# A routing table built by accumulating indirect DMAs instead of one-hot matmuls, in a fused two-block transformer kernel

## The chip, the cores and the metric

The kernel runs on one core of a Trainium2 chip. The metric is the device time of one launch in microseconds (us). The kernel before takes 1685.63 us, the median of three runs (1685.04 to 1687.07).

## The reference, cut to what matters

The program computes one block with a recurrent mixer and an expert layer (PEER), followed by two blocks with attention and a feed-forward layer, for 256 tokens of width 1024, in f32. The change lies in the expert layer. For each token and each of 8 heads, two lists of 128 key scores are cut to their top 16, the 256 sums of pairs are cut to the top 16 again, and a softmax over these gives 16 weights with 16 expert numbers out of 128 * 128.

```
q = (t @ w_q).reshape(n_tok, 8, 2, 128)
sc = einsum("thpk,hpnk->thpn", q, sub_keys)
s_top, i_top = top_k(sc, 16)
cand = s_top[:, :, 0, :, None] + s_top[:, :, 1, None, :]
cand_idx = i_top[:, :, 0, :, None] * 128 + i_top[:, :, 1, None, :]
best, pos = top_k(cand.reshape(n_tok, 8, 256), 16)
idx = take_along_axis(cand_idx.reshape(n_tok, 8, 256), pos)
g = softmax(best)
act = gelu(einsum("phkd,pd->phk", u_tab[idx], t))
out = einsum("phk,phkd->pd", g * act, v_tab[idx])
```

A token uses at most 128 of 16384 experts. The kernel computes all of them densely: with a table W of weights, 128 x 128 x 256 (second index j, first index i, token), mostly zero, the layer is the sum over j of V_j times (W_j * gelu(U_j x)). A block j holds 128 experts; U_j and V_j are 128 x 1024 each.

## The kernel before, in words

**Products.** A matmul operand is split into a rounded part (`high`, made by ScalarE in `take_high`, L823) and the rest (`low`, made by VectorE in `take_low`, L1748), and a product is three matmuls. A piece of weights is 128 x 1024 (512 KB). Pieces go through a ring of four slots (`raw`, `high`, `low`): SyncE's `load` (L612) waits for the `low` of the piece four before, `ahead(p)` on ScalarE and VectorE makes the parts of the piece four after p, and TensorE signals `slot_done`. The order of all pieces is `STREAM`. Each engine executes its instructions, and each queue its issues, in the order written, so a wait holds up all behind it.

**Up to the scores.** The mixer runs in 8 rounds over 8 pieces each. VectorE's `finish` (L1887 to L1890) ends a round (`merged_ready`). Then 8 pieces of `mix_out`, a norm (add L1990, squares L804, transposes L1245), and 16 pieces of `query` in four rounds `it`, of two heads each. In a round the four query projections are followed by 8 score matmuls (L1386), and VectorE does the top-k work of the round (L2030 to L2096) after the lows of the four pieces ahead.

**U blocks before the table.** 24 `NATIVE` blocks run as plain f32 matmuls (L1398) between the rounds, from buffers of their own. 36 `STAGED` blocks run through the ring (`project_in`, L1255 to L1257), 4 before and 32 during the making of the table. Their activations gelu(U_j x) wait in the arena.

**The table.** W is made for 4 tokens at a time in 64 groups: VectorE (L2116, L2121), ScalarE (L976, L982) and GpSimd (L770) build one-hot matrices, and TensorE multiplies them (L1423), 4 matmuls of 128 x 128 a group. ScalarE copies the result to the arena (L998), or VectorE multiplies it into stored activations.

**Experts.** In `expert_step` the other 68 (`LATE`) blocks do V_j (`project_out`, L1305 to L1309) and U_(j+3) (`project_in_halves`, L1275 and L1277) in turn, with a sum (L2163), a gelu (L1017), a multiplication by the table (L2167) and the split of the product (L1025, L1758) for each; 60 more steps do V alone. After the last V comes a norm and the rest of the network.

Of the kernel before, what the change touches and what calls it, by code (L numbers as in the profile page):

```python
# [67 lines left out]
EARLY_OF_ROUND = (4, 4, 4, 12)  # L68
NATIVE = sum(EARLY_OF_ROUND)
LEAD, STAGED = 4, 36  # L70
FIRST_NATIVE = NKEYS - NATIVE
EARLY = NATIVE + STAGED
LATE = NKEYS - EARLY
GROUPS = SEQ // 4
# [6 lines left out]
class Chain:  # L81
# [28 lines left out]
    def link(self, ins):  # L110
# [4 lines left out]

STREAM = [("mix", 8 * KC), ("mix_out", KC), ("query", 16), ("staged", STAGED), ("expert", NKEYS + LATE),
          ("diff_v", KC), ("diff_qk", 16), ("diff_out", KC), ("ffn0", 3 * FF_CHUNKS),
# [70 lines left out]
def piece_staged(k):  # L188

    return Piece("staged", k)  # L190


def staged_block(k):

    return FIRST_NATIVE - 1 - k


def first_staged(n):

    return FIRST_NATIVE - LEAD - n // 2  # L200


def piece_u(j, it=0):

    return Piece("expert", j if j < 3 else 2 * j - 2, it, 8)


def piece_v(j, it=0):

    return Piece("expert", 2 * j + 3, it, 8) if j < LATE - 3 else Piece("expert", j + LATE, it, 4)  # L210
# [28 lines left out]
def build(nc, x, w_mix, w_gate, w_out, w_query, keys, u_tab, v_tab, diff_qk, diff_v, diff_out,  # L239
# [3 lines left out]
    with ctx:  # L243
# [5 lines left out]


# [100 lines left out]
        def weights_of(n, j, j_end):  # L351

            return arena[:, :].rearrange("p (j t) -> p j t", t=SEQ)[:, j:j_end, 4 * n:4 * n + 4].rearrange("p j t -> p t j")

        def coefficients(j, it):

            return coef[j % 2] if j < LATE else at(arena, it * (4 * SEQ) + j * SEQ, SEQ)

        def staged_part(k, lo, hi):

            return part(staged_block(k) * SEQ + lo, hi - lo)

        def staged_bank(k, lo, hi):

            return bank(4 + k % 4, lo, hi - lo)

        def scattered(n):

            return bank(n % 4).rearrange("p (t j) -> p t j", t=4)
# [13 lines left out]
        one_hot = [h_tok[:, 512 * n:512 * n + 512] for n in range(2)]  # L383
        one_hot_w = [h_tok[:, 1024 + 512 * n:1536 + 512 * n] for n in range(2)]
        coef = [h_tok[:, SEQ * n:SEQ * n + SEQ] for n in range(2)]
        u_sum = [h_tok[:, 512 + SEQ * n:512 + SEQ * n + SEQ] for n in range(2)]
        weight = spare[:, :]
        minus_weight = params[:, 0:GROUPS]
        sel_i, sel_j = (yh[:, SEQ * n:SEQ * n + SEQ].bitcast(F32) for n in range(2))

        filler = part(8192, HALF)
# [2182 lines left out]
```

## Time and profile before

| what | us or share |
|---|---|
| median of three runs | 1685.63 |
| time of the profiled execution's span | 1683.6 |
| difference (outside the span, and between executions) | 2.0 |
| TensorE busy | 99% |
| VectorE busy | 77% |
| ScalarE busy | 55% |
| GpSimd busy | 7% |
| granted TensorE clock, mean | 0.999 of 2.4 GHz |

The profiled execution has no other time of its own than its span. PE is TensorE, DVE is VectorE, ACT is ScalarE, POOL is GpSimd, SP is SyncE. The end of a matmul is modelled, and consecutive matmuls overlap, so the pace of TensorE is read from starts and not from durations.

### The profile page before, as it was taken

The page shows a single profiled execution, that of the slowest core. Times are in us where ns is not written, and L with a number is a line of the kernel's source. Part 1 is how long each engine was busy: PE and PEld are TensorE (multiplying, and loading weights), DVE is VectorE, ACT ScalarE, POOL GpSimd, SP SyncE. Part 2 cuts the span into 40 slices and gives each one's busy share as a digit, 9 for nine tenths or more (in the row PEclk, how much of TensorE's full clock was granted, in tenths as well). Part 3 has the DMA queues.
Part 4 walks back from the last instruction along what each step waited for, and adds up shares of the span by engine and source line. Part 5 has one row for each costly group of instructions (what it writes and reads, how often), then busy time and mean ns, then how long its engine had stood idle before and what let it go on. Part 6 is the DMA issues. An engine that isn't in the chain of part 4 may idle for free.

```text
span 1683.6 us, 28949 instructions
## 1 busy us (share of the span) xinstructions
PE 1665.7 (99%) x10094; PEld 1470.5 (87%) x10094; DVE 1302.4 (77%) x2459; ACT 931.8 (55%) x1625; POOL 109.8 (7%) x94
## 2 busy tenths in 40 slices
PE   9999999999999999999999999999999999999998
PEld 8999899999998888888888888898888878888886
DVE  7888789989997666666666666687877877687777
ACT  5666632268875444444444545565655545655554
POOL 1000000035550000000000000010000000000000
PEclk9999999999999999999999999999999999999999
DMA  6556733523336555555556567544665645266663
GB/s 218 181 181 202 251 128 133 197 75 114 113 111 212 187 187 188 188 186 187 188 187 191 193 195 254 166 134 152 201 187 187 200 160 164 89 200 188 187 187 112
DMA packets 84601, 292.96 MB, mean 174 GB/s; under 512 B 11696, under 2 KB 13488, under 8 KB 84144
## 3 DMA queue, kind: packets, MB, share of 16 engines
q1 hardware_dynamic: 82800, 286.54, 52.3%
q10 hardware_dynamic: 1728, 5.45, 0.9%
q8 instruction: 45, 0.74, 0.2%
q14 instruction: 28, 0.23, 0.1%
HBM read 289.33 MB, written 2.10 MB: 173 GB/s over the span
## 4 chain that ended last, share of the span: by engine, by line
PE 87%; issue 7%; DVE 4%; ACT 1%; POOL 0%; DMA 0%; POOLq 0%; DVEq 0%; ACTq 0%
PE ps L1275 16%; PE ps L1305 10%; PE ps L1307 10%; PE ps L1309 10%; PE ps L1277 8%; PE ps L1255 7%; PE ps L1256 7%; PE ps L1257 7%; PE ps L1398 5%; PE ps L1423 3%; PE ps L1288 1%; DVE low L1748 1%; DVE held_low L1748 0%; DVE arena L1817 0%; PE ps L1386 0%
## 5 line engine op out<-in xcount | busy, mean ns | idle before, releaser
L1748 DVE TENSOR_TENSOR low<-raw,high 128x1024 fp32r<-128x1024 f32 x492 | 591.3, 1209 | 184.5 <-ACT high L823 177.6
L823 ACT ACTIVATE high<-raw 128x1024 fp32r<-128x1024 f32 x493 | 513.8, 1046 | 304.4 <-PE ps L1309 132.0
L1275 PE MATMUL ps<-x_parts,high 128*128 128x512 f32 x1216 | 432.9, 398 | 0.0
L1277 PE MATMUL ps<-x_parts,low 128*128 128x256 f32 x1216 | 341.2, 281 | 0.0
L1255 PE MATMUL ps<-x_parts,low 128*128 128x256 f32 x1104 | 317.4, 288 | 1.4 <-DVE x_parts L1864 0.9
L1257 PE MATMUL ps<-x_parts,high 128*128 128x256 f32 x1104 | 312.2, 283 | 0.0
L1256 PE MATMUL ps<-x_parts,high 128*128 128x256 f32 x1104 | 312.2, 283 | 0.0
L1275 PEld LDWEIGHTS ps<-x_parts,high 128*128 128x128 f32 x1216 | 228.4, 188 | 55.1
L1277 PEld LDWEIGHTS ps<-x_parts,low 128*128 128x128 f32 x1216 | 229.5, 189 | 4.0
L1255 PEld LDWEIGHTS ps<-x_parts,low 128*128 128x128 f32 x1104 | 211.5, 192 | 4.1 <-issue 1.4
L1256 PEld LDWEIGHTS ps<-x_parts,high 128*128 128x128 f32 x1104 | 211.6, 192 | 0.1
L1257 PEld LDWEIGHTS ps<-x_parts,high 128*128 128x128 f32 x1104 | 211.5, 192 | 0.0
L1305 PE MATMUL ps<-high,yl 128*128 128x512 f32 x640 | 199.8, 393 | 0.1
L1307 PE MATMUL ps<-low,yh 128*128 128x512 f32 x640 | 198.9, 392 | 0.0
L1309 PE MATMUL ps<-high,yh 128*128 128x512 f32 x640 | 197.3, 389 | 0.0
L1307 PEld LDWEIGHTS ps<-low,yh 128*128 128x128 f32 x640 | 120.1, 188 | 27.6
L1309 PEld LDWEIGHTS ps<-high,yh 128*128 128x128 f32 x640 | 120.1, 188 | 27.0
L1305 PEld LDWEIGHTS ps<-high,yl 128*128 128x128 f32 x640 | 112.9, 188 | 22.3 <-DVE yl L1758 0.5
L770 POOL TENSOR_SCALAR h_tok<-consts,yh,spare 128x128 f32<-128x128 f32 x64 | 87.4, 1372 | 209.0 <-ACT yh L969 149.8
L754 POOL TENSOR_TENSOR stats<-stats 128x1 f32<-128x1 f32 x14 | 7.9, 565 | 1268.0 <-DVE stats L1789 1268.0
L1398 PE MATMUL ps<-arena 128*128 128x256 f32 x384 | 83.5, 379 | 0.0
L1398 PEld LDWEIGHTS ps<-arena 128*128 128x128 f32 x384 | 72.7, 190 | 9.7
(352 smaller groups left out, 2022.3 us busy)
## 6 DMA issues: line engine op xcount, KB each, us to landing
raw<-in_v_tab SPq DMA_DIRECT2D x128, 512.0 KB, 3.4
raw<-in_u_tab SPq DMA_DIRECT2D x104, 512.0 KB, 3.5
raw<-in_ffn_in SPq DMA_DIRECT2D x88, 512.0 KB, 4.1
raw<-in_w_mix SPq DMA_DIRECT2D x56, 512.0 KB, 4.5
raw<-in_ffn_out SPq DMA_DIRECT2D x44, 512.0 KB, 3.5
arena<-in_u_tab SPq DMA_DIRECT2D x24, 512.0 KB, 3.6
raw<-in_w_query SPq DMA_DIRECT2D x16, 512.0 KB, 5.3
raw<-in_diff_qk SPq DMA_DIRECT2D x16, 512.0 KB, 4.3
```

The costliest lines, as they stand in the source:

```text
L770: pool.tensor_scalar(one_hot_w[n % 2][:, 3 * PARTS:4 * PARTS], iota, sel_j[:, t:t + 1], weight[:, t:t + 1], ALU.is_equal, ALU.mult).then_i ...
L823: a.activation(w_high(p, 0, n), cols(raw, p, 0, n), ACT.Copy).then_inc(slot_high[p.slot], 1)
L1255: pe.matmul(dst, left[1], right[0], start=start, stop=False)
L1256: pe.matmul(dst, left[0], right[1], start=False, stop=False)
L1257: return pe.matmul(dst, left[0], right[0], start=False, stop=stop)
L1275: pe.matmul(bank(b).rearrange("p (h t) -> p h t", h=2), cols(high, p, k * PARTS, PARTS), both[:, :, k, :], start=(k == 0), stop=False)
L1277: ins = pe.matmul(bank(b, 0, SEQ), cols(low, p, k * PARTS, PARTS), chunk_of(xh, k), start=False, stop=(k == KC - 1))
L1305: pe.matmul(bank(2 * t + half), src_low[:, xs], w_high(p, half * HALF, HALF), start=first, stop=False)
L1307: pe.matmul(bank(2 * t + half), src_high[:, xs], w_low(p, half * HALF, HALF), start=False, stop=False)
L1309: ins = pe.matmul(bank(2 * t + half), src_high[:, xs], w_high(p, half * HALF, HALF), start=False, stop=stop)
L1398: ins = pe.matmul(bank(4 + early % 4, 0, SEQ), early_u[early % 4][:, k * PARTS:(k + 1) * PARTS], chunk_of(xf, k), start=(k == 0), stop=(k ...
L1748: v.tensor_tensor(w_low(p, 0, n), cols(raw, p, 0, n), w_high(p, 0, n).bitcast(F32), ALU.subtract).then_inc(slot_low[p.slot], 1)
```

## The change

The one-hot matrices, their matmuls, the native blocks and the staged blocks go. A DRAM tensor `routed` (128 x 128 x 256 f32, 16.8 MB) takes the table. GpSimd clears it during the mixer with 32 DMAs of 512 KB, four after each `merged_ready`. VectorE makes in each top-k round the flat index and the weight of each chosen expert (32 per token and round). GpSimd adds them with one indirect DMA for each head, token tile and rank: 256 DMAs, each of 128 single f32 elements, one per partition. Before a head of one token tile, it waits until all DMAs of that tile's earlier heads have landed (two heads may choose the same expert). 64 U blocks run through the ring with `project_in`, 16 behind the four queries of each round, and VectorE's `ahead` calls are written between the steps of the top-k. 64 more U blocks follow with `project_in_halves` (`inner_step`). All 128 V blocks follow all U blocks (`outer_step`), and SyncE loads a 128 KB part of the table for each, after it has waited for all 256 indirect DMAs. The load of the keys (1 MB) moves on SyncE's queue from before `mix_out` to behind it, after a wait for the last `merged_ready`, and so ahead of the query pieces; the store of `h` moves ahead of the U pieces. The softmax is done in each round and not once. The buffer `xf` and its addition (L2011) go.

```
-EARLY_OF_ROUND = (4, 4, 4, 12)
-LEAD, STAGED = 4, 36
+ROUNDS, OF_ROUND = 4, 16
+EARLY = ROUNDS * OF_ROUND
+SCRATCH = 44
+SLOTS = HEADS * 16
+ZERO_PARTS = 32
...
+def block_of(k):
+    return k + SCRATCH if k < NKEYS - SCRATCH else k - (NKEYS - SCRATCH)
```

On SyncE:

```
-            sp.dma_start(keysT, keys).then_inc(keys_loaded, 16)
             for k in range(KC):
                 load(Piece("mix_out", k), w_out[k])
+            sp.wait_ge(merged_ready, KC)
+            sp.dma_start(keysT, keys).then_inc(keys_loaded, 16)
+            for it in range(ROUNDS):
                 for q in range(4 * it, 4 * it + 4):
+                    load(piece_query(q), w_query[q])
                 if it == 0:
                     sp.wait_ge(h_ready, TB)
                     sp.dma_start(h_saved, h_tok[:, :]).then_inc(h_kept, 16)
+                for k in range(it * OF_ROUND, (it + 1) * OF_ROUND):
+                    load(piece_u(k), u_tab[block_of(k)])
...
+            def outer_step(j, it):
                 load(piece_v(j, it), pick(v_tab, it * 4 + j))
+                if j == 0:
+                    for b in range(TB):
+                        sp.wait_ge(scattered[b], 16 * SLOTS)
+                if j >= 4:
+                    sp.wait_ge(coef_ready, it * 4 + (j - 3))
+                sp.dma_start(routed_part[j % 4], pick(routed, it * 4 + j)).then_inc(routed_loaded[j % 4], 16)
```

On GpSimd:

```
+            for c in range(KC):
+                pool.wait_ge(merged_ready, c + 1)
+                for n in range(c * ZERO_PARTS // KC, (c + 1) * ZERO_PARTS // KC):
+                    pool.dma_start(cleared[n], zeros).then_inc(zeroed, 16)
             inverse_roots(1, 2)
+            pool.wait_ge(zeroed, 16 * ZERO_PARTS)
+            for h in range(HEADS):
+                if h % 2 == 0:
+                    pool.wait_ge(chosen_ready, h // 2 + 1)
+                for b in range(TB):
+                    if h >= 1:
+                        pool.wait_ge(scattered[b], 16 * 16 * h)
+                    for n in range(b * SLOTS + 16 * h, b * SLOTS + 16 * h + 16):
+                        pool.indirect_dma_start(entries, bass.IndirectOffsetOnAxis(ap=slot_index[:, n:n + 1], axis=0),
+                                                slot_weight[:, n:n + 1], None, compute_op=ALU.add).then_inc(scattered[b], 16)
```

On TensorE:

```
+            for it in range(ROUNDS):
                 for q in range(0 if it else 2, 4):
+                    project_in(piece_query(4 * it + q), bank(4 + q, 0, SEQ))
+                for k in range(it * OF_ROUND, (it + 1) * OF_ROUND):
+                    project_in(piece_u(k), bank(4 + k % 4, 0, SEQ))
+                    if k % OF_ROUND == 0:
...
+            def inner_step(k, it):
+                project_in_halves(piece_u(k, it), 4 + k % 4)
+            def outer_step(j, it):
                 pe.wait_ge(coef_low, it * 4 + (j + 1))
                 if j < NKEYS - HOLD:
+                    project_out(piece_v(j, it), *y_parts(j, NKEYS), 0, first=(j == 0))
```

On ScalarE, in each round:

```
+                for k in range(it * OF_ROUND, (it + 1) * OF_ROUND):
+                    ahead(piece_u(k))
+                    gelu_early(k)
+                    if k % OF_ROUND == OF_ROUND - 2:
+                        a.wait_ge(shifted_ready, it + 1)
+                        w = slot_weight3[:, :, 32 * it:32 * it + 32]
+                        a.activation(w, w, ACT.Exp).then_inc(exp_ready, 1)
```

On VectorE in each round, behind the top-k steps with `ahead(u[0])` to `ahead(u[14])` between them, and then the new steps behind all rounds:

```
+                    ins = v.tensor_scalar(first, first, 2.0 * PARTS, token[:, b:b + 1], ALU.mult, ALU.add)
+                v.wait_ge(exp_ready, it + 1)
+                link(v.tensor_reduce(sums.rearrange("p (b h) -> p b h", b=TB), weights4, AX.X, ALU.add))
+                link(v.reciprocal(sums, sums))
+                    v.scalar_tensor_tensor(out=index3[:, b, heads], in0=second, scalar=2.0 * PARTS * PARTS, in1=first, op0=ALU.mult, op1=ALU.add)
+                    ins = v.tensor_tensor(weights4[:, b], weights4[:, b], sums[:, 2 * b:2 * b + 2].unsqueeze(2).to_broadcast([PARTS, 2, 16]), ALU.mult)
+                ins.then_inc(chosen_ready, 1)
...
+            def inner_step(k, it):
+                v.tensor_reduce(u_sum[k % 2], halves(4 + k % 4), AX.X, ALU.add).then_inc(u_summed, 1)
+                if k in (NKEYS - 2, NKEYS - 1):
+                    coef_low_part(k - (NKEYS - 2))
+                ahead(p)
+                if k in (NKEYS - 4, NKEYS - 3, NKEYS - 2):
+                    weigh(k - (NKEYS - 4))
+            def outer_step(j, it):
                 if j + 2 < NKEYS:
                     coef_low_part(j + 2, it)
+                if j < NKEYS - 2:
                     ahead(piece_v(j, it))
+                if j + 3 < NKEYS:
+                    weigh(j + 3, it)
```

## Rows read from the trace of the kernel before

**Rows 1.** The page: busy time by engine, then the granted clock in 40 slices.

```profile
PE 1665.7 (99%) x10094; PEld 1470.5 (87%) x10094; DVE 1302.4 (77%) x2459; ACT 931.8 (55%) x1625; POOL 109.8 (7%) x94
...
PEclk9999999999999999999999999999999999999999
```

**Rows 2.** Windows: stretch, its length, busy PE, PEld, DVE, ACT, POOL, clock, DMA share, GB/s.

```profile
25.00:180.00 155.00, 155.00 (x1293) 154.87 (x1291) 136.19 (x244) 104.39 (x154) 0.00 (x0) 1.00 0.58 192
180.00:220.00 40.00, 39.23 (x238) 34.65 (x239) 28.60 (x50) 23.78 (x43) 1.10 (x2) 1.00 0.66 231
220.00:357.00 137.00, 136.53 (x836) 126.26 (x835) 129.73 (x472) 40.82 (x75) 1.26 (x1) 1.00 0.41 143
357.00:507.00 150.00, 149.94 (x1283) 149.51 (x1282) 144.12 (x317) 125.00 (x285) 86.12 (x64) 1.00 0.34 109
507.00:860.00 353.00, 353.00 (x1774) 296.88 (x1773) 243.48 (x321) 172.94 (x254) 0.00 (x0) 1.00 0.59 190
```

**Rows 3.** TensorE's timeline: start, us, line, tile, count; boundaries of blocks.

```profile
220.01 1.95 PE L1386 MATMUL ps<-arena 128*128 128x128 f32 x16
221.80 1.03 PE L1398 MATMUL ps<-arena 128*128 128x256 f32 x4
...
345.22 0.39 PE L1255 MATMUL ps<-x_parts,low 128*128 128x256 f32 x1 [0.47 <-ACT arena L946]
...
353.95 0.82 PE L1410 MATMUL ps<-consts,arena 128*128 128x128 f32 x6
...
507.39 0.40 PE L1275 MATMUL ps<-x_parts,high 128*128 128x512 f32 x1
...
515.87 0.63 PE L1305 MATMUL ps<-high,yl 128*128 128x512 f32 x2
...
655.66 0.64 PE L1305 MATMUL ps<-high,yl 128*128 128x512 f32 x2
...
658.45 0.39 PE L1275 MATMUL ps<-x_parts,high 128*128 128x512 f32 x1
...
1034.88 0.62 PE L1305 MATMUL ps<-high,yl 128*128 128x512 f32 x2
...
1037.60 0.62 PE L1305 MATMUL ps<-high,yl 128*128 128x512 f32 x2
...
1052.16 0.63 PE L1305 MATMUL ps<-high,x_parts 128*128 128x512 f32 x2
```

**Rows 4.** Groups of the page: busy us, mean ns of one.

```profile
L1748 DVE TENSOR_TENSOR low<-raw,high 128x1024 fp32r<-128x1024 f32 x492 | 591.3, 1209 | 184.5 <-ACT high L823 177.6
...
L770 POOL TENSOR_SCALAR h_tok<-consts,yh,spare 128x128 f32<-128x128 f32 x64 | 87.4, 1372 | 209.0 <-ACT yh L969 149.8
L754 POOL TENSOR_TENSOR stats<-stats 128x1 f32<-128x1 f32 x14 | 7.9, 565 | 1268.0 <-DVE stats L1789 1268.0
...
L1398 PE MATMUL ps<-arena 128*128 128x256 f32 x384 | 83.5, 379 | 0.0
```

**Rows 5.** Groups of the window 355 to 506 us.

```profile
L1423 PE MATMUL ps<-h_tok 128*128 128x128 f32 x512 | 62.5, 275 | 0.0
...
L1748 DVE TENSOR_TENSOR low<-raw,high 128x1024 fp32r<-128x1024 f32 x32 | 38.8, 1213 | 0.0
```

**Rows 6.** VectorE's timeline, second top-k round and lows of the next.

```profile
259.76 1.64 DVE L2030 MAX8 arena<-arena 128x8 f32<-128x128 f32 x8
...
287.32 4.62 DVE L1748 TENSOR_TENSOR low<-raw,high 128x1024 fp32r<-128x1024 f32 x4
```

**Rows 7.** GpSimd's one-hot line: duration in ns, min, median and max.

```profile
L770 POOL TENSOR_SCALAR h_tok<-consts,yh,spare x64: 787/1382/2293, 355.7 to 500.8; 128x128 f32<-128x128 f32 x64
```

**Rows 8.** DMA issues: count, KB each, median us from issue to landing.

```profile
raw<-in_w_query SPq DMA_DIRECT2D x16, 512.0 KB, 5.3
...
raw<-in_w_gate SPq DMA_DIRECT2D x8, 128.0 KB, 2.8
arena<-in_keys SPq DMA_DIRECT2D x1, 1024.0 KB, 7.4
...
spare<-in_forget_bias SPq DMA_DIRECT2D x2, 8.0 KB, 3.6
```

**Rows 9.** Timeline before the norm: SyncE's issues, VectorE, ScalarE.

```profile
186.24 7.65 SPq L612 DMA_DIRECT2D raw<-in_w_query  x4
...
189.31 0.43 DVE L1890 SCALAR_TENSOR_TENSOR arena<-arena 128x256 f32<-128x256 f32 x1
...
191.99 1.99 ACT L823 ACTIVATE high<-raw 128x1024 fp32r<-128x1024 f32 x2
...
193.44 2.35 DVE L1748 TENSOR_TENSOR low<-raw,high 128x1024 fp32r<-128x1024 f32 x2
...
196.20 1.37 DVE L1990 SCALAR_TENSOR_TENSOR h_tok<-ps,h_tok 128x512 f32<-128x512 f32 x2 [0.41 <-PE ps L1302]
```

More of the change, by code:

```diff
@@ L184, in later, with piece_query, piece_u @@
         return p
[L188 to L205, printed above, removed]
+def piece_query(q):
+    return Piece(f"query{q // 4}", q % 4)
+def piece_u(k, it=0):
+    return Piece(f"early{k // OF_ROUND}", k % OF_ROUND) if k < EARLY else Piece("inner", k - EARLY, it, 4)
+def block_of(k):
+    return k + SCRATCH if k < NKEYS - SCRATCH else k - (NKEYS - SCRATCH)
 def piece_v(j, it=0):
-    return Piece("expert", 2 * j + 3, it, 8) if j < LATE - 3 else Piece("expert", j + LATE, it, 4)
+    return Piece("outer", j, it, 4)
 def piece_gate(l, n, it=0):
@@ L425, in build @@
         best = part(7744, 64)
-        sel = part(7808, 3 * SEQ)
+        chosen = part(7808, 2 * 64)
         expsum = part(8576, 32)
-        early_u = [part(9216 + D * n, D) for n in range(4)]
-        xf = part(13312, KC * SEQ)
         v_tok = part(0, TB * D)
@@ L1011, in _ @@
[L1011 to L1022 removed]
+                if it == 1:
+                    a.wait_ge(zeroed, 16 * ZERO_PARTS)
@@ new lines, in _ @@
+                    ahead(u[12 + 2 * n])
+                    chain.wait()
+                    chain.step(v.tensor_tensor(eqs4, eqs4, idx4[:, :, n, :].unsqueeze(2).to_broadcast([PARTS, 4, 16, 16]), ALU.mult))
+                    if n == 0:
+                        ahead(u[13])
+                    chain.wait()
+                    chain.step(v.tensor_reduce(places4[:, n], eqs4, AX.X, ALU.add))
+                chain.wait()
+                for b in range(TB):
+                    first, second = (chosen[:, 64 * n + 32 * b:64 * n + 32 * b + 32] for n in range(2))
+                    ins = v.tensor_scalar(first, first, 2.0 * PARTS, token[:, b:b + 1], ALU.mult, ALU.add)
@@ new lines, in _ @@
+                chain.step(ins)
+                v.wait_ge(exp_ready, it + 1)
+                sums = expsum[:, 0:4]
+                link(v.tensor_reduce(sums.rearrange("p (b h) -> p b h", b=TB), weights4, AX.X, ALU.add))
+                link(v.reciprocal(sums, sums))
+                for b in range(TB):
+                    first, second = (chosen[:, 64 * n + 32 * b:64 * n + 32 * b + 32] for n in range(2))
+                    v.scalar_tensor_tensor(out=index3[:, b, heads], in0=second, scalar=2.0 * PARTS * PARTS, in1=first, op0=ALU.mult, op1=ALU.add)
+                    ins = v.tensor_tensor(weights4[:, b], weights4[:, b], sums[:, 2 * b:2 * b + 2].unsqueeze(2).to_broadcast([PARTS, 2, 16]), ALU.mult)
```

573 lines of the change are left out of this document (195 added, 378 removed).

## The prediction

> **What bounds the kernel now.** I read the page first: TensorE is busy 99% of the span, at full clock in every slice [rows 1]. A busy TensorE need not be a TensorE at its pace, so I then read windows by stage: its share is full from 25 us to 860 us, VectorE's reaches 144 of 150 us while the table is made, and the 16 DMA engines are busy 34% to 66% [rows 2]. Last I read the pace from starts [rows 3]. The reader is to see that blocks follow each other without gaps, so that the time of the expert layer is the sum of TensorE's blocks, from the first score matmul at 220.01 to the first matmul of the next stage at 1052.16: 832.2 us.
>
> **What TensorE does in the 832.2 us.** From [rows 3]: three `project_in` blocks take 353.95 - 345.22 = 8.73, so 2.91 each; three `project_in_halves` blocks 515.87 - 507.39 = 8.48, so 2.83; a V block among U blocks 658.45 - 655.66 = 2.79, and among V blocks 1037.60 - 1034.88 = 2.72. A round's scores take 221.80 - 220.01 = 1.79. The native blocks take 83.5 [rows 4], 3.48 each. The one-hot matmuls take 62.5 by the group's busy time [rows 5]; with their overlaps out, the table stage of 150 us [rows 2] less its 32 staged blocks (93) leaves 57.
>
> **The change on TensorE.** The new order holds 4 * 1.79 = 7.2 of scores, 12 queries and 64 early U blocks at 2.91 (221.2; the first round's four queries lie before 220.01), 64 U blocks at 2.83 (181.1) and 128 V blocks. Among V blocks alone 2.72 applies: 348.2. VectorE has 0.42 more to do there for each V (the multiplication by the table), some 2.1 us of 2.72, and ScalarE 1.5, so they hide. The sum is 757.7, and the saving 832.2 - 757.7 = 74.5. It consists of 57 for the one-hots, 24 * (3.48 - 2.91) = 14 for the native blocks, and small terms. With V at 2.79 it is 65.
>
> **VectorE in a round.** A round on TensorE is 20 * 2.91 + 1.79 = 60.0. VectorE's top-k work is 287.32 - 259.76 = 27.6 [rows 6]. The new index and softmax steps, some ten short ones, I estimate at 2 from that stretch. 20 lows at 1.21 [rows 4] are 24.2. The sum, 53.8, fits into 60.0. Following the order step by step, with scores ready 6 us after the fourth query (one U block, the scores, ScalarE's copies), each low comes 2 us or more before TensorE needs it, the tightest being those for the next round's queries. So the round costs no stall, and its chosen slots are ready about 53 us after the fourth query. If that cover goes, each us too much costs 4 us in four rounds.
>
> **The moved key load, a cost.** The keys now wait on SyncE for the last `merged_ready`, and the four query loads stand behind them. The last `finish` ends at 189.7, where SyncE issued the first query at 186.24 [rows 9]. ScalarE and VectorE split queries 0 and 1 (191.99 and 193.44) in their order before the norm's first add at 196.20, so a late query holds up the norm, on which TensorE waits. Queued now at 189.7 are 1 MB of keys, 1 MB of two queries, and beside them the last 2 MB of clearing. Below: query 1 lands 5.3 after its issue at 190.5 [rows 8], its split takes 2.3, and VectorE is free at 198.1, 2 late. Above: 4 MB at the rate that 231 GB/s in a 0.66 share makes for full engines, 350 [rows 2], takes 12, and with a latency of 2 and the split VectorE is free at 206, 10 late. I take 6.
>
> **Clearing.** 32 * 0.52 = 16.8 MB in the mixer add about 95 GB/s to 192 in a share of 0.58 [rows 2], so 0.87. Loads have several us of lead there. I take 1, with 0 and 10 as ends. GpSimd has nothing else to do then but two small steps of the norm, and the first of these comes behind the add at 196.20, over 6 us after the last clears can start.
>
> **The scatter, the unknown.** The trace before has no DMA from GpSimd. Work that must be done: 256 DMAs. The first 64 can begin at 53 us after the fourth query. TensorE ends all U blocks 7.2 + 221.2 + 181.1 = 409 after it. From the last landing to the first V there are the table's load (2.8, as the 128 KB gate load, [rows 8]) and what VectorE and ScalarE have queued around `weigh(0)`, about 5 (two sums, two lows, the splits). The last DMA itself lands in about 2.8. So there are 409 - 53 - 5 - 2.8 - 2.8 = 345 us for 256, or 1.35 each, and everything above goes one to one into the end. Later rounds leave more: 64 DMAs in the last 185 us. The waits for earlier heads hide, as 16 DMAs of the other tile lie between.
>
> What is one DMA's price c on GpSimd? Below: a GpSimd instruction on one column took 0.565 [rows 4]. Above: one at a time from issue to landing, 2.8 [rows 8]; then 256 take 717, and V starts 372 late. Between them lies the 128-column one-hot, 1.37 beside a VectorE that is hardly ever idle [rows 7]. A column of 128 entries is nearer to the small instruction in data, but 128 descriptors are more work than one pass; I take 1.2, so 307 us and no stall. On the DMA engines 128 packets of a few bytes are little: the 8 KB broadcast landed in 3.6, against 2.8 for 128 KB [rows 8].
>
> **A rule that speaks against it.** The one-hot on GpSimd took between 0.79 and 2.29 for the same work [rows 7], so something held it up for over a us at times. The Trainium skill (SBUF — State Buffer, section "SBUF: two separate sides") states that GpSimd and VectorE share a port pair as an exclusive lock, and that descriptors of a DMA from GpSimd can't be written while VectorE holds it in a 2-port mode; a VectorE op with two SBUF inputs blocks only GpSimd ops that read SBUF. By that the spread agrees, and whether an indirect DMA counts as reading is open. The Trainium skill (DMA: Bandwidth & Descriptors, section "Anatomy of one DMA — SWDGE (gpsimd) path") fits 2.0 us for one small DMA, mostly receipt; were that paid in series, V would start 167 us late and the time be 1785.
>
> **The sum.** -74.5 + 6 + 1 = -67.5. The span before is 1683.6, so 1616.1; the median stands 2.0 above that span, so 1618. 0.2% is 3.4 us, about what a measurement of this kernel can tell from no change.
>
> **The rivals.**
> - A partly late scatter: c between 1.35 and 1.61. The stall is 256c - 345, and the gain is used up at (345 + 67.5) / 256 = 1.61. For it: the one-hot's 1.37 [rows 7] gives a stall of 6 and 1624; c = 1.5 gives 39 and 1657.
> - A scatter that sets the time: c above 1.61, the case on the other side. The mechanism is one DMA's descriptor work on GpSimd, held up by VectorE. In the inner stage VectorE runs one two-operand low of 1.21 in each block of 2.83; if GpSimd gets only the remaining 1.62, my 1.2 becomes 2.1, 538 us in all, a stall of 193 and 1811. At c = 2.0 it is 167 and 1785. For it: the spread of [rows 7]. Against: an indirect DMA reads a single column, and VectorE was busy 144 of 150 us there [rows 2], while in the inner stage a sum and a low make about 1.9 of 2.83.
> - VectorE as the bound in the rounds: with 0.5 us more for each of its 25 large ops in a round (20 lows, 5 of the top-k) the 53.8 become 66, 6 over the 60.0, or 24 in four rounds, and 1642. Against: the low was no longer beside GpSimd's work (1.21 in the table stage [rows 5] and 1.21 over all [rows 4]).
> - That the change does not remove the work cannot be: the one-hots and natives are gone from the program, and TensorE has nothing hidden to put in their place.
>
> **How the numbers follow.** Forecast (c up to 1.35): 0.50, with a range of its own from 1606 to 1628. Partly late: 0.12, of which 0.09 is faster and 0.03 within 0.2%. VectorE bound: 0.05, faster. Scatter bound: 0.33, slower. So faster 0.64, same 0.03, slower 0.33. The range begins at 1606 (no cost of the key load and of clearing, 1611, and a shade for faster V blocks), and ends at 1760, which is c = 1.9; above lie 0.17 and below 0.03.
>
> **What would show it.** Right: V starts at about 636 us in the new trace (220 + 409 + 7), with no gap of TensorE before it; rounds 60 us apart; the last indirect DMA lands before 628; the gap before the norm's transposes grows by 6; V blocks 2.72 apart. Wrong: SyncE waits for GpSimd at `outer_step(0)`, TensorE idle between the last U and the first V, and GpSimd's DMAs back to back all the way from the first round. Then the price c has failed, not the sum of the blocks. If TensorE waits for lows in the rounds, the VectorE sum has failed.

## The result and the profile after

The changed kernel takes 1918.99 us (1917.12 to 1919.34, 4 runs) beside 1685.97 (4 runs) of the kernel before. The ratio is 1.138, 95% interval [1.136, 1.139]: slower. The forecast was 1618, with a range up to 1760, so the forecast and its range both missed. Below, a time without a range is that of one run; runs of one kernel lie 2 to 4 us apart here. The profiled execution has a span of 1915.3 us, 231.7 more than before.

The page of the changed kernel: busy time of engines, then tenths by slice, what it gives of the chain, and the group of the indirect DMAs. It answers to [rows 1].

```profile
PE 1633.3 (85%) x9800; PEld 1405.8 (73%) x9800; DVE 1244.2 (65%) x2274; ACT 878.6 (46%) x1431; POOL 537.7 (28%) x319
PE   9999799999999500006999999999999999999998
POOL 1100007888888888881000000000100000000000
PEclk9999999999999855557999999999999999999999
PE 28%; POOL 26%; issue 19%; DVE 12%; ACT 9%; DMA 4%; ACTq 1%; DVEq 1%; SPq 0%; POOLq 0%
L752 POOL DMA_INDIRECT routed<-h_tok x256 | 497.1, 1942 | 145.0 <-issue 77.8
```

TensorE has a hole of four slices and its clock falls in them to 0.5, the lower of its two levels; GpSimd, which had next to nothing to do, is on the chain of waits with 26% of the span. Its 256 indirect DMAs take 1.94 us each, and 77.8 us more go by between them ("issue", 0.30 each). Where the hole lies, TensorE's timeline shows, with the boundaries of its stages (it answers to [rows 3]):

```profile
243.79 1.95 PE L1313 MATMUL ps<-arena 128*128 128x128 f32 x16
...
879.24 1.22 PE L1222 MATMUL ps<-high,yl 128*128 128x512 f32 x2 [231.26 <-DVE yl L1640]
...
886.25 0.61 PE L1222 MATMUL ps<-high,yl 128*128 128x512 f32 x2
887.61 0.61 PE L1222 MATMUL ps<-high,yl 128*128 128x512 f32 x2
...
1283.05 0.63 PE L1222 MATMUL ps<-high,x_parts 128*128 128x512 f32 x2
```

The first scores start at 243.79; one U block of 2.91 lies ahead of them, so the fourth query ends at 240.9. The U blocks end at 879.24 - 231.26 = 647.98, the V stage lasts from 879.24 to 1283.05. The releaser named is VectorE's `yl`, but VectorE stood idle too; who waited for what is in SyncE's list of waits:

```profile
SPq L647 <- DMA routed<-h_tok: 239.4, 1, 239.4
```

SyncE waits at `outer_step(0)` for the last indirect DMA before it loads the first block of the table. The windows (PE, weight loads, VectorE, ScalarE, GpSimd, then clock, DMA share, GB/s; they answer to [rows 2]) are those of the mixer, the rounds, the U blocks after the rounds, the hole, and the V blocks:

```profile
25.00:210.00 185.00, 177.23 (x1376) 172.16 (x1375) 148.16 (x264) 113.58 (x168) 17.25 (x32) 0.99 0.72 257
240.00:480.00 240.00, 240.00 (x1972) 238.26 (x1972) 205.95 (x558) 125.36 (x183) 162.83 (x77) 1.00 0.67 178
480.00:640.00 160.00, 160.00 (x908) 138.68 (x907) 108.68 (x114) 76.87 (x113) 142.94 (x57) 1.00 0.66 180
700.00:869.00 169.00, 0.00 (x0) 0.00 (x0) 0.00 (x0) 0.00 (x0) 141.08 (x92) 0.50 0.24 0
900.00:1200.00 300.00, 290.31 (x1157) 209.23 (x1156) 190.78 (x288) 131.15 (x192) 0.00 (x0) 1.00 0.68 210
```

In the U stage TensorE is as full as foretold; in the hole nothing runs but GpSimd; and in the V blocks TensorE's share is under the whole, which is a second loss. GpSimd's counts say how fast the scatter goes: 57 DMAs in 160 us, 92 in 169 us. The ranges of their durations (ns: min, median, max) by stretch:

```profile
L752 POOL DMA_INDIRECT routed<-h_tok x77: 1536/2320/3150, 294.0 to 479.7; - x77
L752 POOL DMA_INDIRECT routed<-h_tok x60: 1543/2522/2592, 479.7 to 645.5; - x60
L752 POOL DMA_INDIRECT routed<-h_tok x108: 1543/1543/1562, 669.5 to 867.3; - x108
```

With all other engines idle one takes 1.54, beside the U blocks after the rounds 2.52, and in the rounds anything from 1.54 to 3.15. With the gaps of 0.30 that is one per 1.85 us alone, (479.7 - 294.0) / 77 = 2.41 in the rounds, and (647.98 - 479.7) / 60 = 2.80 after them, which is very nearly one per U block.

**Where the 231.7 us come from.** The span was to be 1616.1 and is 1915.3, 299.2 more. The terms, each measured less foretold:

| | foretold | measured | off by |
|---|---|---|---|
| fourth query ends later than before by | 7 | 240.9 - 220.0 = 20.9 | +13.9 |
| U stage | 409 | 407.1 | -1.9 |
| TensorE idle ahead of the first V | 0 | 231.3 | +231.3 |
| V stage | 348.2 | 403.8 | +55.6 |
| the rest, to the end | 631.4 | 632.3 | +0.9 |

They add up to 299.8. Against before, the same terms are 20.9 + (407.1 + 231.3 + 403.8 - 832.2) + 0.9 = 231.8.

**The V stage.** ScalarE and VectorE, timelines of one block of the changed kernel:

```profile
1003.12 0.42 ACT L948 ACTIVATE yh<-arena 128x256 fp32r x1 [1.72 <-DVE arena L2024]
1003.45 1.04 ACT L805 ACTIVATE high<-raw 128x1024 fp32r<-128x1024 f32 x1
1006.21 0.42 ACT L948 ACTIVATE yh<-arena 128x256 fp32r x1 [1.72 <-DVE arena L2024]
...
1003.58 0.42 DVE L1640 TENSOR_TENSOR yl<-arena,yh 128x256 fp32r<-128x256 f32 x1 [0.57 <-ACT yh L948]
1004.52 1.23 DVE L1630 TENSOR_TENSOR low<-raw,high 128x1024 fp32r<-128x1024 f32 x1 [0.52 <-ACT high L805]
1005.67 0.42 DVE L2024 TENSOR_TENSOR arena<-arena,h_tok 128x256 f32 x1
```

Both engines are idle for part of each block, and still they set the pace: ScalarE's `yh` waits for the multiply by the table (L2024), the weight's high part follows it on ScalarE, the low (L1630) waits for that, and the multiply stands behind the low in VectorE's order. One turn of this loop is 1006.21 - 1003.12 = 3.09 here, and a V block takes 3.13 on average, where TensorE needs 2.72.

**The start.** The norm's first add and the split ahead of it, and the group of weight splits on ScalarE between 25 and 215 us with what it waited for; it answers to [rows 9]:

```profile
214.17 1.06 ACT L805 ACTIVATE high<-raw 128x1024 fp32r<-128x1024 f32 x1 [2.77 <-DMA raw<-in_w_query]
...
216.40 1.28 DVE L1875 SCALAR_TENSOR_TENSOR h_tok<-ps,h_tok 128x512 f32<-128x512 f32 x2
...
L805 ACT ACTIVATE high<-raw 128x1024 fp32r<-128x1024 f32 x55 | 56.8, 1054 | 67.5 <-DMA raw<-in_w_mix 33.0 <-PE ps L1174 23.2 <-DMA raw<-in_w_query 8.8
```

The add comes at 216.40, 20.2 after its place in [rows 9]. ScalarE waits 8.8 us for the queries (the price foretold for the key load was 6, between 2 and 10), but also 33.0 us for the mixer's own weights, whose loads run beside the clearing; some 12 of these reach the end, as the mixer's last `finish` ends at 201.9 and not at 189.7.

### The profile page after: what moved, and what is told of

Same layout as the page of the kernel before. It is cut to its first block, busy times and chain, and to the rows that moved or that the text cites. A ratio compares the mean times of both kernels' runs of the same rounds, so it can differ in the third digit from the quotient of the medians.

```text
span 1915.3 us, 28883 instructions
## 1 busy us (share of the span) xinstructions
PE 1633.3 (85%) x9800; PEld 1405.8 (73%) x9800; DVE 1244.2 (65%) x2274; ACT 878.6 (46%) x1431; POOL 537.7 (28%) x319
## 4 chain that ended last, share of the span: by engine, by line
PE 28%; POOL 26%; issue 19%; DVE 12%; ACT 9%; DMA 4%; ACTq 1%; DVEq 1%; SPq 0%; POOLq 0%
POOL routed L752 26%; PE ps L1192 8%; ACT high L805 7%; PE ps L1194 4%; DVE arena L2024 3%; DVE low L1630 3%; PE ps L1222 2%; PE ps L1224 2%; PE ps L1226 2%; DMA raw<-in_w_mix 2%; PE ps L1172 2%; PE ps L1174 2%; PE ps L1173 2%; PE ps L1205 1%; DMA raw<-in_w_query 1%
## 5 line engine op out<-in xcount | busy, mean ns | idle before, releaser
L805 ACT ACTIVATE high<-raw 128x1024 fp32r<-128x1024 f32 (+1 forms) x517 | 536.8, 1044 | 543.5 <-DMA raw<-in_v_tab 234.3
L1630 DVE TENSOR_TENSOR low<-raw,high 128x1024 fp32r<-128x1024 f32 (+1 forms) x516 | 621.7, 1210 | 175.7 <-ACT high L805 171.5
L752 POOL DMA_INDIRECT routed<-h_tok x256 | 497.1, 1942 | 145.0 <-issue 77.8
L1192 PE MATMUL ps<-x_parts,high 128*128 128x512 f32 x1184 | 419.6, 398 | 0.0
L1172 PE MATMUL ps<-x_parts,low 128*128 128x256 f32 x1328 | 379.1, 285 | 8.0 <-DVE low L1630 7.1
L1173 PE MATMUL ps<-x_parts,high 128*128 128x256 f32 x1328 | 376.4, 283 | 0.0
L1174 PE MATMUL ps<-x_parts,high 128*128 128x256 f32 x1328 | 376.3, 283 | 0.0
L1194 PE MATMUL ps<-x_parts,low 128*128 128x256 f32 x1184 | 332.3, 281 | 0.0
L1172 PEld LDWEIGHTS ps<-x_parts,low 128*128 128x128 f32 x1328 | 255.4, 192 | 10.8 <-DVE low L1630 8.1
L1192 PEld LDWEIGHTS ps<-x_parts,high 128*128 128x128 f32 x1184 | 222.4, 188 | 54.7
L1173 PEld LDWEIGHTS ps<-x_parts,high 128*128 128x128 f32 x1328 | 255.5, 192 | 0.0
L1174 PEld LDWEIGHTS ps<-x_parts,high 128*128 128x128 f32 x1328 | 255.4, 192 | 0.0
L1194 PEld LDWEIGHTS ps<-x_parts,low 128*128 128x128 f32 x1184 | 223.6, 189 | 1.5
L2024 DVE TENSOR_TENSOR arena<-arena,h_tok 128x256 f32 (+1 forms) x128 | 53.7, 419 | 230.4 <-DMA h_tok<-routed 230.4
L948 ACT ACTIVATE yh<-arena 128x256 fp32r (+1 forms) x124 | 51.9, 418 | 214.5 <-DVE arena L2024 211.7
```

The lines of the kernel that those rows point to most:

```text
L752: pool.indirect_dma_start(entries, bass.IndirectOffsetOnAxis(ap=slot_index[:, n:n + 1], axis=0), slot_weight[:, n:n + 1], None, compute_op ...
L805: a.activation(w_high(p, 0, n), cols(raw, p, 0, n), ACT.Copy).then_inc(slot_high[p.slot], 1)
L1172: pe.matmul(dst, left[1], right[0], start=start, stop=False)
L1173: pe.matmul(dst, left[0], right[1], start=False, stop=False)
L1174: return pe.matmul(dst, left[0], right[0], start=False, stop=stop)
L1192: pe.matmul(bank(b).rearrange("p (h t) -> p h t", h=2), cols(high, p, k * PARTS, PARTS), both[:, :, k, :], start=(k == 0), stop=False)
```

## Experiments

Three losses had to be told apart: the scatter, the order in the V stage, and the start.

**The order of the V stage.** `v_order` swaps two steps of VectorE:

```diff
             def outer_step(j, it):
                 if j + 2 < NKEYS:
                     coef_low_part(j + 2, it)
-                if j < NKEYS - 2:
-                    ahead(piece_v(j, it))
                 if j + 3 < NKEYS:
                     weigh(j + 3, it)
+                if j < NKEYS - 2:
+                    ahead(piece_v(j, it))
```

> Only VectorE's order in the V steps is changed: the multiplication by the table stands before the low of the piece ahead. In the changed kernel a V block takes 3.08 us. Theory A: this is a loop of ScalarE and VectorE (split of the product, rounded part of the piece, its low, the multiplication, and back to the split: 0.42 + 1.04 + 1.23 + 0.42 us), and the order breaks it: V blocks 2.72 apart, 128 * 0.36 = 46 less, about 1873. Rival B: the table's loads or memory make TensorE slower; then V stays at 3.08 and the time at 1919.

Measured: 1870.26 us (1868.79 to 1871.91), ratio 1.110 [1.108, 1.111]. TensorE's timeline and window in the V stage of `v_order`:

```profile
882.40 1.22 PE L1222 MATMUL ps<-high,yl 128*128 128x512 f32 x2 [231.13 <-DVE yl L1640]
...
1234.71 0.63 PE L1222 MATMUL ps<-high,x_parts 128*128 128x512 f32 x2
...
900.00:1200.00 300.00, 300.00 (x1325) 248.43 (x1324) 219.09 (x331) 150.61 (x221) 0.00 (x0) 1.00 0.76 243
```

The stage takes 352.3 us instead of 403.8, TensorE is full in it, and VectorE's busy time has gone up with the pace: it was never short of time. Only the order of two steps differs, so the loop was the cause. The price of 2.72 per V holds in this order (348.2 foretold; about 2.9 of the other 4.1 are the slow first matmuls below).

**The scatter left out.** `few_adds` issues 16 of the 256 indirect DMAs, the first one of each head and tile:

```diff
                     if h >= 1:
-                        pool.wait_ge(scattered[b], 16 * 16 * h)
-                    for n in range(b * SLOTS + 16 * h, b * SLOTS + 16 * h + 16):
+                        pool.wait_ge(scattered[b], 16 * h)
+                    for n in range(b * SLOTS + 16 * h, b * SLOTS + 16 * h + 1):
```

> Leaves out 240 of the 256 indirect DMAs (the table misses 15 of 16 entries). Theory A: the wait for them is all that they cost, so the 231 us of TensorE's wait go and the first V comes within 1 us of the last U; V blocks stay at 3.08; time 1919 - 231 = 1687. Rival B: the adds also slow the U blocks or the loads; then the U stage of 407 us gets shorter too, and the time falls below 1680.

Measured: 1684.53 us. TensorE's first V matmul in `few_adds`:

```profile
647.68 0.62 PE L1222 MATMUL ps<-high,yl 128*128 128x512 f32 x2
```

V follows U without a gap, the U stage is as long as with 256 DMAs, and a V block still takes 3.13 us on average. So the scatter costs TensorE nothing but the hole: 1919 - 1684.5 = 234.5 us for 231.3 us of it and the clock behind it.

**What one indirect DMA costs: its entries.** `half_rows` gives each DMA 64 entries instead of 128, at the same count:

```diff
-bass.IndirectOffsetOnAxis(ap=slot_index[:, n:n + 1], axis=0), slot_weight[:, n:n + 1]
+bass.IndirectOffsetOnAxis(ap=slot_index[0:64, n:n + 1], axis=0), slot_weight[0:64, n:n + 1]
```

> Each indirect DMA takes the first 64 partitions only (half of the table's entries are left out). An indirect DMA takes 1.54 us on GpSimd while VectorE is idle, plus 0.30 to the next. Theory A: the time is descriptors, one per entry, so it falls to 0.8 to 1.0, and beside VectorE's work to 1.7 or less; the wait for the adds falls from 231 to below 60. Rival B: a fixed cost of the instruction, then it stays above 1.4 and the time is 1900 or more.

Measured: 1838.46 us. Durations in `half_rows` in the hole, and in the U blocks after the rounds:

```profile
L752 POOL DMA_INDIRECT routed<-h_tok x72: 1407/1411/1426, 665.1 to 786.8; - x72
L752 POOL DMA_INDIRECT routed<-h_tok x85: 1407/1411/1990, 478.6 to 638.8; - x85
```

Half the entries save 0.13 of 1.54 us. A line through these two points, an estimate, gives 2 ns for each entry and some 1.3 us that no entry changes. By the duration theory A has fallen. Yet the time fell by 80 us, where rival B had 19 at most and 256 * 0.13 is 34: after the rounds the median went from 2.52 to 1.41, as if alone. So it was not the amount of work beside them that had made them 2.52 long; something there hung on a period. That became the question. Whether fewer DMAs with more entries each would be cheaper is not shown: a kernel with 16 of them, of 16 columns each, gave no time.

**What holds a DMA up: operations of VectorE.** `vector_in_wait` puts three kinds of operations of VectorE into the hole, each linked to the one before:

```diff
                 ahead(p)
+                if k == NKEYS - 4:
+                    for _ in range(60):
+                        link(v.tensor_tensor(yl[:, :], xh[:, 0:HALF].bitcast(F32), xl[:, 0:HALF].bitcast(F32), ALU.add))
+                    for _ in range(130):
+                        link(v.tensor_copy(spare[:, :], xh[:, 0:SEQ].bitcast(F32)))
+                    for _ in range(60):
+                        link(v.tensor_tensor(yl[:, :], bank(0), xl[:, 0:HALF].bitcast(F32), ALU.add))
```

> Adds work to VectorE in the stretch in which it waits for the table and nothing is loaded: 60 additions of two SBUF operands (128 x 512, 0.69 us each), then 130 copies SBUF to SBUF (128 x 256), then 60 additions of a PSUM and an SBUF operand (128 x 512). The results are not used. In the changed kernel an indirect DMA takes 1.54 us there, against 2.5 beside VectorE's lows. Theory A: a port that GpSimd shares with VectorE is held, so the DMA gets longer beside at least one of the three kinds, to 2 us or more, first of all beside two SBUF operands as in the lows. Rival B: it was the loads of weights on the same DMA engines; then it stays at 1.54 beside all three.

Measured: 1925.37 us. The durations in `vector_in_wait` beside the sums of two SBUF operands, beside the copies, and beside the sums with one operand in PSUM; then the copies' own durations:

```profile
L752 POOL DMA_INDIRECT routed<-h_tok x17: 1874/1875/1877, 649.5 to 684.4; - x17
L752 POOL DMA_INDIRECT routed<-h_tok x26: 1550/1550/1882, 686.6 to 733.3; - x26
L752 POOL DMA_INDIRECT routed<-h_tok x22: 1542/1542/1543, 735.1 to 773.9; - x22
...
L2043 DVE COPY spare<-x_parts x130: 293/295/465, 687.0 to 734.8; 128x256 f32<-128x256 f32 x130
```

Of the three kinds only the sums of two SBUF operands hold an indirect DMA up, and all DMAs beside them are of one length, 1.87 (theory A had said 2 or more). Each ends 1.42 after the end of the sum in which it began. The sums that read PSUM hold up nothing: 1.54, at whatever point of a sum a DMA begins. By this, where the rule of the Trainium skill (SBUF — State Buffer, section "SBUF: two separate sides") left open whether an indirect DMA counts as a GpSimd operation that reads SBUF, it behaves as one that does.

The copies show less than that. Beside them a DMA takes 1.55, but the two run in step: a DMA starts every 1.86 us, in which just five copies pass, and always 0.02 after the start of a copy. So only this one meeting was tried, and in it the copies are the ones that get longer: 25 of the 130 take 0.45 or more where most take 0.29, about one for each DMA. The warning of the same section of the Trainium skill that copies of fp32 within SBUF keep GpSimd from writing descriptors is thus neither shown nor refuted; the copies here are short, and longer ones were not run.

**What holds a DMA up: traffic.** `loads_in_wait` has SyncE copy 60 blocks of `u_tab` within DRAM during the hole, two at a time.

```diff
                 if j == 0:
+                    for n in range(60):
+                        if n >= 2:
+                            sp.wait_ge(copied[n % 2], 16 * (n // 2))
+                        sp.dma_start(junk[n], u_tab[n]).then_inc(copied[n % 2], 16)
                     for b in range(TB):
                         sp.wait_ge(scattered[b], 16 * SLOTS)
```

> Adds 60 DMAs of 512 KB from the U table to an unused DRAM tensor on SyncE's queue, two at a time, in the stretch in which VectorE and all loads are idle. Theory A (VectorE's port): an indirect DMA stays at 1.54 us beside them. Rival B (DMA engines or memory): it rises to 2.3 us or more.

Measured: 1919.94 us. Window and durations in `loads_in_wait`:

```profile
660.00:860.00 200.00, 0.00 (x0) 0.00 (x0) 0.00 (x0) 0.00 (x0) 167.01 (x109) 0.50 0.63 131
...
L758 POOL DMA_INDIRECT routed<-h_tok x109: 1542/1542/1561, 660.0 to 859.6; - x109
```

With the DMA engines at a share of 0.63, about that of the U stage (0.66), the indirect DMAs take 1.54 as before. Traffic is not it, as far as copies within DRAM can stand for loads into SBUF; `split_lows` below has these loads beside DMAs of 1.54.

**Is it a phase lock?** The timelines of GpSimd and VectorE in the changed kernel, after the rounds:

```profile
561.67 2.46 POOL L752 DMA_INDIRECT routed<-h_tok  x1 [0.30 <-issue]
564.43 2.58 POOL L752 DMA_INDIRECT routed<-h_tok  x1 [0.30 <-issue]
...
561.48 1.23 DVE L1630 TENSOR_TENSOR low<-raw,high 128x1024 fp32r<-128x1024 f32 x1 [0.31 <-ACT high L805]
...
564.37 1.23 DVE L1630 TENSOR_TENSOR low<-raw,high 128x1024 fp32r<-128x1024 f32 x1 [0.37 <-ACT high L805]
```

A DMA starts 0.19 after a low has begun and ends 1.42 after that low's end (564.13 against 562.71); the next starts 0.30 later, at 564.43, just after the next low has begun at 564.37, and is held up again. A DMA alone needs 1.54 + 0.30 = 1.84 of the 2.83 of a block, but the low delays each one by just so much that the next meets the next low. The rule holds beyond this pair: after 480 us 57 DMAs are held up, and all 57 end 1.41 to 1.44 after the low that was running when they began. The DMA of 64 entries, 0.13 shorter, slips out: it starts before the next low, and a low that begins behind it does not hold it up.

The same trace tells about the rounds, where VectorE has the top-k steps too. Of the 77 DMAs there 21 take 1.54, and 49 end 1.41 to 1.44 after the end of an operation with two SBUF operands: 43 after a low, 6 after a step of the top-k (L1997, L2000). The three of 3.15 all begin in the top-k's sum L1958 and outlast also the low behind it:

```profile
323.65 3.15 POOL L752 DMA_INDIRECT routed<-h_tok  x1 [0.30 <-issue]
...
322.90 1.21 DVE L1958 TENSOR_TENSOR arena<-arena 128x1024 f32<-128x1024 f32 x1
324.02 1.22 DVE L1630 TENSOR_TENSOR low<-raw,high 128x1024 fp32r<-128x1024 f32 x1
```

If a DMA after the rounds is held up because it meets the low of each block, a shorter low should free the whole one too. `query_first` is the base for this; it also takes back part of the start:

```diff
+            for q in range(2):
+                load(piece_query(q), w_query[q])
             sp.wait_ge(merged_ready, KC)
             sp.dma_start(keysT, keys).then_inc(keys_loaded, 16)
             for it in range(ROUNDS):
-                for q in range(4 * it, 4 * it + 4):
+                for q in range(4 * it if it else 2, 4 * it + 4):
```

> The V order of before, and the loads of queries 0 and 1 ahead of the wait and the keys on SyncE's queue. Theory A: the norm's first add no longer waits for query 1 (its load landed 14 us late), 8 us less than with the V order alone, the rest of the later start being the clearing: 1865. Rival B: the last clears alone hold the queries up, then it is within 3 us of the V order alone.

Measured: 1863.45 us, 6.8 less than `v_order`, near theory A's 8: first scores at 241.05, and ScalarE's waits for queries down to 4.7. `split_lows` takes that kernel and makes two lows of each in the U stage; `parted_lows` does so after the rounds only, with the block's sum from PSUM between the halves. The edit of `split_lows`:

```diff
                 v.wait_ge(slot_high[p.slot], p.count)
-                v.tensor_tensor(w_low(p, 0, n), cols(raw, p, 0, n), w_high(p, 0, n).bitcast(F32), ALU.subtract
-                                ).then_inc(slot_low[p.slot], 1)
+                first = 0
+                if start_of("query0") <= p.n < start_of("outer"):
+                    first = HALF
+                    v.tensor_tensor(w_low(p, 0, first), cols(raw, p, 0, first), w_high(p, 0, first).bitcast(F32), ALU.subtract)
+                v.tensor_tensor(w_low(p, first, n - first), cols(raw, p, first, n - first), w_high(p, first, n - first).bitcast(F32), ALU.subtract
+                                ).then_inc(slot_low[p.slot], 1)
```

> In the U stage every low of 1,024 columns on VectorE becomes two of 512, back to back; otherwise query_first (1863.5 us). Theory A: an indirect DMA reads its index only when VectorE is not in an operation on two SBUF operands, and with one low per block it falls into step with the lows, one DMA per block of 2.82 us. If the short pause between two operations back to back is enough, a DMA is held up for at most 0.65 us, ends before the next low and gets out of step: period about 2.1 us in the stretch after the rounds, some 75 DMAs where there were 57, and about 1830 us. If the pause is not enough, nothing changes (2.52 us each, 1863). Rival B: the longer DMAs of that stretch come from the stage's traffic, and the lows only mark its beat: no change either, here and in parted_lows.

> In the blocks after the rounds the low is two of 512 columns with the sum of 512 columns from PSUM (0.69 us) between them; otherwise query_first (1863.5 us). Theory A: each half holds a DMA up for at most 0.65 us and the sum from PSUM for nothing, so that it gets out of step with the blocks: mean period 2.1 to 2.3 us in that stretch, 70 to 78 DMAs for 57, and 1825 to 1840 us. Rival B (the traffic of the stage makes them 2.5 us long): still 57 DMAs and 1863 us.

Measured: `split_lows` 1799.44 us, `parted_lows` 1815.11. Durations from 480 to 640 us in `query_first`, `split_lows` and `parted_lows`, in this order:

```profile
L754 POOL DMA_INDIRECT routed<-h_tok x57: 2451/2524/2592, 479.8 to 638.1; - x57
```

```profile
L754 POOL DMA_INDIRECT routed<-h_tok x85: 1542/1543/2184, 479.8 to 639.6; - x85
```

```profile
L754 POOL DMA_INDIRECT routed<-h_tok x84: 1542/1542/1907, 479.3 to 639.6; - x84
```

Timelines of GpSimd and VectorE in `split_lows`, in a round and after the rounds:

```profile
309.59 2.46 POOL L754 DMA_INDIRECT routed<-h_tok  x1 [0.30 <-issue]
...
563.59 1.71 POOL L754 DMA_INDIRECT routed<-h_tok  x1 [0.30 <-issue]
...
309.37 0.67 DVE L1635 TENSOR_TENSOR low<-raw,high 128x512 fp32r<-128x512 f32 x1
309.96 0.68 DVE L1636 TENSOR_TENSOR low<-raw,high 128x512 fp32r<-128x512 f32 x1
...
563.19 0.69 DVE L1635 TENSOR_TENSOR low<-raw,high 128x512 fp32r<-128x512 f32 x1 [0.37 <-ACT high L807]
563.80 0.69 DVE L1636 TENSOR_TENSOR low<-raw,high 128x512 fp32r<-128x512 f32 x1
```

The work of VectorE is the same, and slightly more of it; 85 DMAs go through where 57 did, and the time falls by 64 us. The DMA that starts at 563.59, within the first half, ends 1.42 after that half's end (565.30 against 563.88), though the second half runs from 563.80 on. So it is held up by 0.17 and not by both halves, and all 28 that began in a first half after the rounds went so. It needs no pause between the two: in the trace the halves overlap by 0.08. In the rounds it is not so sure. The DMA at 309.59 begins 0.22 after the first half has and ends 1.42 after the second (312.05 against 310.64); of the 32 that began in a first half there, 21 waited for the second. What decides this the runs do not show.

Theory A is shown after the rounds: as the loads of weights run there as before, rival B, the stage's traffic, has fallen. The gain is larger than theory A said for both (1830 for `split_lows`, 1825 to 1840 for `parted_lows`), as nearly all DMAs of that stretch are as long as alone. In the rounds the median came down only from 2.32 to 1.83, and 85 instead of 78 went through by 480 us.

**The start, and the change without its scatter.** `bare` leaves out 240 of the adds as `few_adds` does, has both edits above (V order, two queries first), and moves the clearing behind the norm's root on GpSimd, four at a time, so that it runs in the first round:

```diff
-            for c in range(KC):
-                pool.wait_ge(merged_ready, c + 1)
-                for n in range(c * ZERO_PARTS // KC, (c + 1) * ZERO_PARTS // KC):
-                    pool.dma_start(cleared[n], zeros).then_inc(zeroed, 16)
             inverse_roots(1, 2)
+            for n in range(ZERO_PARTS):
+                if n and n % 4 == 0:
+                    pool.wait_ge(zeroed, 16 * n)
+                pool.dma_start(cleared[n], zeros).then_inc(zeroed, 16)
```

> Leaves out 240 of the 256 indirect DMAs, as before, and mends the rest: the multiplication before the low in the V steps, two query loads ahead of the keys on SyncE, and the clearing of the table in the first top-k round and not in the mixer. Theory A: what is left is the sum of TensorE's blocks that I forecast without the adds, less the 7 of key load and clearing: 1611. If the clearing beside the first round costs as much as in the mixer (12 us), 1623. Rival B: the U stage or V stage has another loss, and it stays above 1635.

Measured: 1623.73 us (1623.11 to 1625.89), ratio 0.964 [0.962, 0.965]. ScalarE's group of splits between 25 and 215 us in `bare`:

```profile
L807 ACT ACTIVATE high<-raw 128x1024 fp32r<-128x1024 f32 x59 | 62.1, 1057 | 51.4 <-PE ps L1176 47.5 <-PE ps L1208 3.3
```

ScalarE waits for TensorE alone there, so no load is late in the mixer any more; the norm's first add comes at 196.47 and the scores at 223.17. Less the U block now ahead of them that is 220.3, against 220.0 before: both costs of the start are gone. But the clearing takes its price where it now runs. From the first scores to the first V (638.83) it is 415.7 us, where the changed kernel has 647.98 - 243.79 = 404.2, so 11.5 more. Without its scatter the change is thus worth 1621.3 - 1683.6 = -62.3, where the forecast's sum said -67.5; with the 11.5 of the clearing taken out it is -73.8, where its blocks said -74.5.

`late_clears` is that place of the clearing with all 256 adds:

> query_first with the 32 clearing DMAs moved from the mixer's end to the first round, all 256 indirect DMAs kept. The clearing was seen to cost the first scores some 18 us at the mixer's end and the first rounds some 12 us in bare; but here TensorE waits for the last indirect DMA, which can't start before the clearing is through. Theory A (only the last indirect DMA sets the time): scores start at 223, the first indirect DMA about 15 to 18 us earlier than in query_first, and the time is 1863 less that, 1846 to 1850 us. Rival B: the clearing beside the first round holds up the chosen slots by as much as it gave back, or runs past them: 1856 us or more.

Measured: 1868.45 us, 5 more than `query_first`. That is not far above the spread of single runs, but the trace shows the same. GpSimd's timeline in `late_clears`:

```profile
291.34 2.10 POOL L742 DMA_DIRECT2D routed<-arena  x4 [10.49 <-DMA routed<-arena]
298.56 1.65 POOL L754 DMA_INDIRECT routed<-h_tok  x1 [5.12 <-DMA routed<-arena]
```

Rival B holds: the scores start 18 us earlier (223.0), but each group of four clears takes some 12 us from one to the next, the last is issued only at 291.34, and the first indirect DMA starts at 298.56 instead of 291.27. As long as the scatter sets the time, only the start and the pace of GpSimd's queue count.

**The best version.** `split_lows` again, timed as `best_of_after`:

> The kernel of split_lows (lows of 512 columns in the U stage, queries 0 and 1 ahead of the keys, the multiply ahead of the low in the V stage), now timed against the kernel before for an interval. Every theory that is left puts it at 1799 us within 3, so at a ratio of 1.067 to 1.069: still slower than before, since its indirect DMAs alone need 256 x 1.84 = 472 us from 290 on, and end some 115 us after the U stage at best.

Measured: 1802.67 us (1801.62 to 1805.55), ratio 1.070 [1.068, 1.072]. It is 116 us faster than the changed kernel and still 117 slower than before.

## Why the prediction was wrong

**The step that failed is the price c of one indirect DMA**, taken as 1.2 us between 0.565 and 2.8. The duration alone is 1.54 and the gap behind it 0.30, so 1.85; beside the stage as it was written it was 574.9 / 256 = 2.25. The formula around it held: chosen slots 53 us after the fourth query (first DMA at 294.0, so 53.1), 10.6 us from the last DMA to the first V (868.8 to 879.24 is 10.4), and a stall of 256 * 2.25 - 345 = 231, as measured. Even c alone lies above the break-even of 1.61. What went wrong in choosing 1.2 is that the column of 128 entries was held against instructions that compute, and that no term stood for the 0.30 between two DMAs. The two bounds were in the text, and the rival "a scatter that sets the time" had the outcome's mechanism, held-up descriptor work at one low per block, and priced it at c = 2.1 and 1811; it had 0.33. Its range was too short: with the forecast's other terms, c = 2.25 gives 1616 + 231 = 1847, and 1760 was c = 1.9.

**The mechanism of the rival was half right.** It had VectorE's low take the time away from the DMA, which would leave 1.62 per block. The runs showed that a low holds up only a DMA that begins while it runs, that the meeting repeats for want of 0.1 us, and that after the rounds the same low in two halves costs next to nothing. The argument against it, that VectorE's share was only 1.9 of 2.83, looked at the wrong thing: a share says nothing on who meets whom.

**The V stage at 2.72 was missed by 55.6.** "They hide" was said of sums, 2.1 and 1.5 of 2.72. The sums were about right (219.09 and 150.61 of 300 us in `v_order`, so 1.99 and 1.37 a block); that the pieces form a loop over two engines was not looked at. `v_order` put it back to 352.3.

**The start was missed by 13.9.** The key load behind `merged_ready` cost about what was said; `bare` shows that none of it need be paid, and `query_first`, with the clearing left where it was, gets about half of it back at the scores. The clearing had been taken at 1, with 10 as the far end. It cost 12 in the mixer, where the DMA share went to 0.72 and ScalarE waited 33 us for weights; the 0.87 foretold for the share, taken as no lateness, was not even reached.

**Right:** the U stage (407.1 against 409), the rounds 59.4 apart where 60.0 was said, and without a wait for VectorE, the tail, and the saving on TensorE, by `bare` and the estimate of 11.5 for its clearing. The rival of VectorE as the bound in the rounds fell: TensorE is full there.

What stays open: what the 1.3 us of an indirect DMA that no entry changes consist of, and why some DMAs in the rounds wait for two operations in a row and others for one. That steps of the top-k hold DMAs up is read from the trace and was not tried apart.

## What to carry to other kernels

Before work goes from a full engine to an idle one, count the instructions that the idle engine issues in a row and price one with its gap; 256 of them at 1.85 us are 473 us, however little each moves. A sum of busy times per block shows that engines can keep up only if no chain runs through both of them within the block: follow one block around the loop. And where durations in a stretch are all equal and near to the period of something else, look for a phase lock before counting contention; a small cut in either (a low in two halves, 64 us) tells. The same holds for a test: two loops that run in step, as the copies and the DMAs did, show one meeting only.

## What the runs showed of the hardware

- An indirect DMA of 128 entries takes GpSimd 1.54 us and one of 64 entries 1.41, and 0.30 lie between one and the next.
- A VectorE operation with two SBUF operands that is running when it begins holds it up until the operation's end, and it ends 1.42 after that: 17 of 17 beside sums of 0.69 us, 57 of 57 beside lows of 1.23 after the rounds. Of two such operations in a row it waited for the first alone in 28 of 28 cases after the rounds of `split_lows`, and for both in 21 of 32 in the rounds.
- Sums of an SBUF and a PSUM operand don't hold it up (1.54), and neither does DMA traffic within DRAM at a share of 0.63. Beside fp32 copies of 0.29 us within SBUF it takes 1.55, and about one copy for each DMA takes 0.45 or more.
- After 231 us without work TensorE runs at 0.5 of its clock, its lower level (1.2 GHz). The first three tile steps behind the hole (the third ends at 886.25) take 886.25 - 879.24 = 7.0 us, where three at the full clock take 3 * 1.36 = 4.1: some 2.9 us in all.
- 16.8 MB of clearing cost some 12 us at either of two places where loads of weights ran beside it: in the mixer, at a share of 0.72, and in the first round.
